# Sub-norm statistics of the second attention by token in columns, and three places changed in the order of a round

## The chip, the cores and the metric

One core of one Trainium2 chip runs the whole kernel. The metric is the device time of one execution in microseconds; before the change the median of three runs is 1058.67 us (1057.43 to 1059.17). The engines are TensorE (PE; its weight loads are shown as PEld), VectorE (DVE), ScalarE (ACT), GpSimd (POOL) and SyncE (SP, which issues all DMAs). Each runs its own instructions in their written order and waits for the others on semaphores, which the kernel places by hand.

## The reference

Two transformer blocks on 512 tokens of width 1024, float32. The change lies in the second block, in the part that mixes two kinds of attention. The differential half has 4 heads of 128 values:

```python
p = jax.nn.softmax(sc, axis=-1)              # two score maps per head
a = p[:, :, 0] - lam * p[:, :, 1]            # causal, with ALiBi slopes
d_out = einsum('bhqk,bhkd->bhqd', a, v)
d_out = rms_norm(d_out, diff_subln) * (1.0 - lambda_init)   # over the 128 values of a head, eps 1e-6
d_out = d_out * silu(dg)
```

The other half (8 "moba" heads of 64 values; with 512 tokens its block choice falls away and it is plain causal softmax attention) has no such norm: its output is `softmax(...) v * silu(mg)`. Both are joined and multiplied by `w_out_2`. The norm over a head's 128 values, for each token, is what the kernel below calls the sub-norm.

## The kernel before, in words

Activations lie transposed: features on the 128 partitions, the 512 tokens along the free side. Each float32 product is made of three products of split numbers (high and low parts; L442 to L444), so one "piece" of a projection is three matmuls of 128x512. Weights come in units of 128x1024; for each unit ACT makes the high part (L1047), POOL the low part (L2173), PE then multiplies 8 pieces.

The second attention goes over 8 chunks c = 0 to 7 of 128 features. Even chunks are differential heads (two score maps, "head" 0 and 1 of the code, joined into one before the values), odd chunks are two moba heads. A round of the main loop takes an even chunk c and the odd chunk c + 1 and prepares c + 2: three full rounds (c = 0, 2, 4), and then a tail in which chunk 6 and 7 end beside the first pieces of the output projection (`out_chunks`). A round lasts some 42 us. No planner orders the work: each engine's block writes its order out by hand, and the loops `for c in range(0, KC, 2)` of PE, ACT, DVE and POOL are the four queues that the change touches.

What they do for a chunk:
- `scores2(c, part)` on PE makes the scores in three parts, `biased(c, part)` on DVE adds the slopes and takes the row maximum (L1994, L1997), `exponentials(c, part)` on ACT (L1413) takes the exponentials in place in `s2` and their sums in `den`.
- Even chunks only: `joined(c, blocks)` on DVE (L2007, L2009, L2014) adds the second map, times a factor by token, to the first.
- `transposes(c, head)` on PE (L870) turns the probabilities into bank PT; `high_probs` (ACT, L1425) and `low_probs` (DVE, L1566) split them; `values2(c, head)` on PE multiplies them with the values into bank OUT.
- Even chunks then: `raw_out` on DVE copies bank OUT into `att2`, `square_out` on ACT squares it into `d_sq`. `square_sum(c)` on PE sums the squares over the 128 partitions with a matrix of ones (L931), which leaves the sum in every partition of bank OUT, and adds the epsilon term, spread as `rx_d`, with four more products by the identity (L933). `variance` on DVE copies that to `d_v`, `first_root` on ACT takes exp(-0.5 ln v) (L1445, L1447), `root` on DVE makes one Newton step and the scaling (four operations, L1562, L2088, L2091, L2094), all on 128x512. POOL multiplies by the gate (`gated_out`, L2347) and later makes the low part of the result (`mixed_low`).
- Odd chunks: `den_rows` on PE (L902) spreads the reciprocal sums into bank PT, `gate_row` on DVE multiplies them into the gate, `gated` gives the output.
- The gate of chunk c is a projection of 8 pieces (`gate_part`), drained by DVE (`gate2_drain`), clamped by POOL (L2336), its sigmoid made by ACT (L1431 to L1435) and multiplied by POOL (`gate_silu`, L2341).

The order of a round around the change, before it. PE: transposes(c+1, 0), square_sum(c), half of value projection c+3, scores2(c+2, 0), transposes(c+1, 1), scores2(c+2, 1), other half of value projection, scores2(c+2, 2), values2(c+1, 0), 5 gate pieces, values2(c+1, 1), den_rows(c+1), 3 gate pieces, and then transposes(c+2) of the next round, which wait for `joined(c+2)`. DVE: variance(c), low_probs(c+1, 0), biased(c+2, 0), biased(c+2, 1), value_drain(c+3), root(c), biased(c+2, 2), low_probs(c+1, 1), joined (two blocks), gate_row(c+1), joined (two blocks), gate2_drain(c+2). ACT: high_probs(c+1, 0), gate_sigmoid(c+1), a weight unit, gate_sigmoid(c), exponentials(c+2, 0), first_root(c), exponentials(c+2, 1). POOL, unchanged: gate_silu(c+1), the low part of a weight unit, gate_silu(c), and then gated_out(c), which waits for `root(c)`.

The arrays `ncol` (128x4x4), `den`, `rden`, `fac`, `rx_d`, `d_sq`, `att2`, `s2` lie in SBUF, `ps` is PSUM. `V.wait()` makes DVE wait for its own last recorded instruction.

Of the kernel before, what the change touches and what calls it, by code (L numbers as in the profile page):

```python
# [14 lines left out]
P = 128  # L15
# [63 lines left out]
def two_layer_block(nc, xT, vecs, wstream, outT):  # L79
    with ExitStack() as ctx:  # L80
# [161 lines left out]
        def out_weights(t):  # L242
# [46 lines left out]
            sem("out_read"), sem("raw_copied"), sem("dsq_ready"), sem("dss_ready"), sem("dvar_ready"),  # L289
            sem("drs_ready"), sem("d_final"), sem("att2_final"), sem("mixed_ready"))  # L290
        pool_held, gap_zeroed = sem("pool_held"), sem("gap_zeroed")
        stored = sem("stored")
# [146 lines left out]
        def _(pe):  # L439
# [433 lines left out]
            def values2(c, head=0):  # L873
# [8 lines left out]
                if head == 0:  # L882
                    pe.wait_ge(v2_lo_ready, max(c + 1, 2))
                    if not is_diff(c):
                        pe.wait_ge(gap_zeroed, 2)
                        pe.wait_ge(dvar_ready, c // 2 + 1)
                    elif c:
                        pe.wait_ge(out_read, c // 2)
# [8 lines left out]
            def den_rows(c):  # L897

                pe.wait_ge(rx_ready, c + 1)
                pe.wait_ge(ptl_ready, tq_of(c, 1) + 1)  # L900
                for b in range(TB):
                    mm = pe.transpose(ps[:, PT_BANK, b * P:(b + 1) * P], rx_m[:, b, :], ident[:, :])  # L902
                mm.then_inc(row2_ready, 1)
# [21 lines left out]
            def square_sum(c):  # L925

                if c >= KC:
                    return
                pe.wait_ge(dsq_ready, c // 2 + 1)
                pe.wait_ge(rx_ready, c + 1)  # L930
                pe.matmul(ps[:, OUT_BANK, :], ones[:, :], d_sq[:, :], start=True, stop=False, skip_group_check=True)  # L931
                for b in range(TB):
                    mm = pe.matmul(ps[:, OUT_BANK, b * P:(b + 1) * P], rx_d[:, b, :], ident[:, :], start=False,  # L933
                                   stop=b == TB - 1, skip_group_check=True)
                mm.then_inc(dss_ready, 1)

            def out_chunks(t, first, last):
# [46 lines left out]
            for c in range(0, KC, 2):  # L984
# [19 lines left out]
                if c + 2 < KC:  # L1004
                    square_sum(c)
                    value_half(c + 3, 0)
                    scores2(c + 2, 0)
                    transposes(c + 1, 1)
                    scores2(c + 2, 1)
                    value_half(c + 3, 1)  # L1010
                    scores2(c + 2, 2)
                    values2(c + 1, 0)
                    gate_part(c + 2, 0, 5)
                    values2(c + 1, 1)
                    den_rows(c + 1)
                    gate_part(c + 2, 5, KC)

            square_sum(KC - 2)
            pe.wait_ge(g_drained, KC)
            out_chunks(0, 0, KC - 2)  # L1020
            transposes(KC - 1, 1)
            values2(KC - 1, 0)
# [16 lines left out]
        def _(act):  # L1039
# [402 lines left out]
            def first_root(c):  # L1442

                act.wait_ge(dvar_ready, c // 2 + 1)
                A.do(act.activation(d_y[:, :], d_v[:, :], ACT.Ln))  # L1445
                A.wait()
                act.activation(d_y[:, :], d_y[:, :], ACT.Exp, scale=-0.5).then_inc(drs_ready, 1)  # L1447

# [48 lines left out]
            for c in range(0, KC - 2, 2):  # L1497
                if c:
                    high_probs(c - 1, 1)
                    exponentials(c, 2)  # L1500
                    high_mixed(c - 2)
                    split_unit(v_unit(c + 2))
                    split_unit(g_unit(c + 1))
                    stage_v2(c + 1)
# [11 lines left out]
                high_probs(c + 1, 0)  # L1516
                gate_sigmoid(c + 1)
                split_unit(g_unit(c + 2))
                gate_sigmoid(c)
                exponentials(c + 2, 0)  # L1520
                first_root(c)
                exponentials(c + 2, 1)
                stage_qk2(c + 3)

            high_probs(KC - 3, 1)
            exponentials(KC - 2, 2)
            split_unit(g_unit(KC - 1))
# [8 lines left out]
            square_out(KC - 2)  # L1536
            high_probs(KC - 1, 0)
            gate_sigmoid(KC - 2)
            split_unit(U_W2 + 1)
            first_root(KC - 2)  # L1540
            gate_sigmoid(KC - 1)
# [11 lines left out]
        def _(dve):  # L1553
# [465 lines left out]
            def den_small(c):  # L2019
# [4 lines left out]
                if is_diff(c):  # L2024
                    V.do(dve.scalar_tensor_tensor(out=den[:, 0, 0, :], in0=den[:, 0, 0, :], scalar=P * EPS, in1=den[:, 0, 0, :],
                                                  op0=ALU.mult, op1=ALU.mult))
# [3 lines left out]
            def den_spread(c):  # L2030
# [4 lines left out]
                dve.wait_ge(nb_used, 16)  # L2035
                if is_diff(c):
                    r = den[:, 0, 0, :].rearrange("p (b o) -> p b o", o=1).to_broadcast([P, TB, P])
                    dve.tensor_copy(rx_d[:, :, :], r).then_inc(rx_ready, 1)
                else:
                    r = den[:, 1, :, :].rearrange("p h (b o) -> p b h o", o=1).to_broadcast([P, TB, 2, 64])  # L2040
                    dve.tensor_copy(by_heads(rx_m[:, :, :]), r).then_inc(rx_ready, 1)

# [36 lines left out]
            def variance(c):  # L2079

                dve.wait_ge(dss_ready, c // 2 + 1)
                ts(d_v[:, :], ps[:, OUT_BANK, :], 1.0 / P, ALU.mult).then_inc(dvar_ready, 1)

            def root(c):

                dve.wait_ge(drs_ready, c // 2 + 1)
                V.do(tt(d_sq[:, :], d_y[:, :], d_y[:, :], ALU.mult))
                V.do(dve.scalar_tensor_tensor(out=d_y[:, :], in0=att2[:, 0, :], scalar=small[:, 7:8], in1=d_y[:, :],  # L2088
                                              op0=ALU.mult, op1=ALU.mult))
                V.wait(back=1)  # L2090
                V.do(dve.scalar_tensor_tensor(out=d_sq[:, :], in0=d_sq[:, :], scalar=-0.5, in1=d_v[:, :],  # L2091
                                              op0=ALU.mult, op1=ALU.mult))
                V.wait()
                dve.scalar_tensor_tensor(out=att2[:, 0, :], in0=d_sq[:, :], scalar=1.5, in1=d_y[:, :],  # L2094
                                         op0=ALU.add, op1=ALU.mult).then_inc(d_final, 1)

# [30 lines left out]
            for c in range(0, KC, 2):  # L2127
# [4 lines left out]
                den_small(c)  # L2132
                den_spread(c)
                biased(c + 1, 1)
# [11 lines left out]
                variance(c)  # L2146
                low_probs(c + 1, 0)
                biased(c + 2, 0)
                biased(c + 2, 1)
                value_drain(c + 3)  # L2150
                root(c)
                biased(c + 2, 2)
                low_probs(c + 1, 1)
                joined(c + 2, (3, 2))
                gate_row(c + 1)
                joined(c + 2, (0, 1))
                gate2_drain(c + 2)
# [344 lines left out]
```

## Time and profile before

| | |
|---|---|
| median of three runs | 1058.67 us |
| time of the profiled execution | 1057.33 us |
| its span (first to last instruction) | 1055.5 us |
| PE busy | 1032.9 us, 98% of the span |
| DVE, ACT, POOL busy | 514.8, 458.9, 516.1 us |
| granted clock of PE, mean | 1.00 |
| chain that ended last, share of PE | 87% |
| DMA | 91.03 MB, mean 86 GB/s |

PE is the engine to look at; the others are busy for about half of the span. The starts of two neighbouring rows of a timeline give what the first cost the engine; the durations of matmuls overlap. The profiled time is 1.83 us above its span, and the median is 1.34 us above the profiled time. Times in a timeline are microseconds from the start of the span.

### The profile page before, as it was taken

The numbers are of one execution on the slowest core, as the hardware profiler recorded it, in microseconds if no ns is written. First come the engines' busy times: TensorE is split into PE (matmuls) and PEld (weight loads), VectorE is DVE, ScalarE is ACT, GpSimd is POOL, SyncE is SP. The second block draws the span as 40 slices with busy tenths as digits, with TensorE's granted clock in tenths as the row PEclk, the third lists the DMA queues.
The fourth block names the chain that finished last, engine by engine and source line by source line (L and its number), as shares of the span: only waits on it lengthen the run. The fifth ranks groups of instructions, "written<-read, shape, count | busy, mean of one in ns | idle before, by whom it ended". The sixth has DMA issues, their size and how long they took to land.

```text
span 1055.5 us, 13360 instructions
## 1 busy us (share of the span) xinstructions
PE 1032.9 (98%) x4926; PEld 849.3 (80%) x4926; DVE 514.8 (49%) x833; ACT 458.9 (43%) x667; POOL 516.1 (49%) x300
## 2 busy tenths in 40 slices
PE   7999999999999999999999999999999999999998
PEld 5888887788888787888888888887888877777787
DVE  6899763544362465343434311003624176675731
ACT  5322345788753334332323322223353357476540
POOL 3444554933434514444444446445276544675562
PEclk9999999999999999999999999999999999999999
DMA  7233231112142312232222323334122211111112
GB/s 241 87 100 100 80 100 40 60 41 80 61 158 97 124 40 80 99 99 98 88 93 99 99 100 104 109 106 139 41 80 79 81 61 41 61 45 56 40 60 80
DMA packets 25965, 91.03 MB, mean 86 GB/s; under 512 B 3008, under 2 KB 3136, under 8 KB 25792
## 3 DMA queue, kind: packets, MB, share of 16 engines
q1 hardware_dynamic: 25920, 90.42, 25.5%
q8 instruction: 30, 0.49, 0.2%
q14 instruction: 15, 0.12, 0.0%
HBM read 88.31 MB, written 2.10 MB: 86 GB/s over the span
## 4 chain that ended last, share of the span: by engine, by line
PE 87%; DVE 5%; issue 3%; ACT 3%; POOL 1%; DMA 0%; SPq 0%; POOLq 0%; DVEq 0%; ACTq 0%
PE ps L442 26%; PE ps L443 25%; PE ps L444 25%; PE ps L846 1%; PE ps L870 1%; POOL w_lo L2173 1%; DVE s L2014 1%; PE ps L484 1%; PE ps L568 1%; PE ps L588 1%; DVE sp L1687 1%; ACT soft L1137 1%; ACT soft L1135 1%; PE ps L582 1%; ACT soft L1133 1%
## 5 line engine op out<-in xcount | busy, mean ns | idle before, releaser
L2173 POOL TENSOR_TENSOR w_lo<-w_raw,w_hi 128x1024 fp32r<-128x1024 f32 x146 | 346.9, 2377 | 428.2 <-ACT w_hi L1047 379.0
L1047 ACT ACTIVATE w_hi<-w_raw 128x1024 fp32r<-128x1024 f32 (+1 forms) x140 | 146.4, 1045 | 290.1 <-PE ps L444 290.0
L442 PE MATMUL ps<-a_hi,w_hi 128*128 128x512 f32 x560 | 223.4, 399 | 13.0 <-DVE w_lo L1566 7.2
L444 PE MATMUL ps<-a_hi,w_lo 128*128 128x512 f32 x560 | 219.0, 391 | 0.0
L443 PE MATMUL ps<-a_lo,w_hi 128*128 128x512 f32 x560 | 218.8, 391 | 0.0
L442 PE MATMUL ps<-b_hi,w_hi 128*128 128x512 f32 x408 | 159.3, 391 | 1.1 <-POOL w_lo L2173 0.8
L444 PE MATMUL ps<-b_hi,w_lo 128*128 128x512 f32 x408 | 158.8, 389 | 0.0
L443 PE MATMUL ps<-b_lo,w_hi 128*128 128x512 f32 x408 | 158.7, 389 | 0.0
L442 PEld LDWEIGHTS ps<-a_hi,w_hi 128*128 128x128 f32 x560 | 105.6, 189 | 39.0 <-issue 8.7
L444 PEld LDWEIGHTS ps<-a_hi,w_lo 128*128 128x128 f32 x560 | 105.5, 188 | 22.7
L443 PEld LDWEIGHTS ps<-a_lo,w_hi 128*128 128x128 f32 x560 | 105.7, 189 | 20.7
L442 PEld LDWEIGHTS ps<-b_hi,w_hi 128*128 128x128 f32 x408 | 76.6, 188 | 17.7 <-POOL w_lo L2173 1.2
L443 PEld LDWEIGHTS ps<-b_lo,w_hi 128*128 128x128 f32 x408 | 76.6, 188 | 15.8
L444 PEld LDWEIGHTS ps<-b_hi,w_lo 128*128 128x128 f32 x408 | 76.6, 188 | 15.8
L1649 DVE SCALAR_TENSOR_TENSOR ps<-u_pad,vec,ps 128x512 f32<-128x512 f32 x112 | 75.5, 748 | 0.0
L442 PE MATMUL ps<-h_hi,w_hi 128*128 128x512 f32 x176 | 68.5, 389 | 0.0
L443 PE MATMUL ps<-h_lo,w_hi 128*128 128x512 f32 x176 | 68.5, 389 | 0.0
L444 PE MATMUL ps<-h_hi,w_lo 128*128 128x512 f32 x176 | 68.5, 389 | 0.0
L1562 DVE TENSOR_TENSOR up_h<-up_u,up_s 128x512 f32<-128x512 f32 x22 | 49.5, 2248 | 21.5 <-ACT up_s L1306 21.3
L1562 DVE TENSOR_TENSOR up_u<-ps,scale_row 128x512 f32<-128x512 f32 x22 | 15.2, 690 | 83.4 <-PE ps L444 83.4
L1562 DVE TENSOR_TENSOR sq_f<-sq_f 128x512 f32<-128x512 f32 x13 | 9.8, 751 | 82.5 <-ACT sq_f L1330 81.9
L1413 ACT ACTIVATE s<-s,smax 128x384 f32<-128x384 f32 (+2 forms) x64 | 35.2, 552 | 17.2 <-DVE smax L1997 17.2
(324 smaller groups left out, 1600.1 us busy)
## 6 DMA issues: line engine op xcount, KB each, us to landing
w_raw<-weights SPq DMA_DIRECT2D x159, 512.0 KB, 3.3
resid<-x_t SPq DMA_DIRECT2D x8, 256.0 KB, 5.6
resid<-x_t SPq DMA_DIRECT2D x1, 2048.0 KB, 9.5
out_t<-out_sb SPq DMA_DIRECT2D x8, 256.0 KB, 2.0
w_raw<-weights SPq DMA_DIRECT2D x2, 256.0 KB, 4.6
vec<-vecs SPq DMA_DIRECT2D x1, 220.0 KB, 8.2
vec<-vecs SPq DMA_DIRECT2D x1, 4.0 KB, 1.8
```

Of the source, the lines that this page charges most:

```text
L442: pe.matmul(out, s_hi, m_hi, start=first, stop=False, skip_group_check=True)
L443: pe.matmul(out, s_hi, m_lo, start=False, stop=False, skip_group_check=True)
L444: return pe.matmul(out, s_lo, m_hi, start=False, stop=last, skip_group_check=True)
L484: pe.matmul(ps[:, 5, :], tri[:, :], src, start=True, stop=True, skip_group_check=True)
L568: pe.matmul(z_of(h)[:, o:o + (TB - j) * P], k[r, key], q[r, j * P:T], start=j != 3 and t == 0, stop=False, skip_group_check=True)
L582: pe.matmul(z[:, w], tri[:, :], parts[:, w], start=False, stop=False, skip_group_check=True)
L588: mm = pe.matmul(z[:, o:o + width], neg_ones[:, :], parts[:, Z_COL[j2]:Z_COL[j2] + width], start=False, stop=False, skip_group_check=True)
L1047: act.activation(w_hi[:, k % 2, 0:width], w_raw[:, k, 0:width], ACT.Copy).then_inc(hi_ready, 1)
L1413: e = act.activation(s2[:, head, w], s2[:, head, w], ACT.Exp, scale=-1.0, bias=smax[:, head, b:b + 1], accum_out=den[:, kind_of(c), half_o ...
L1562: return dve.tensor_tensor(out, in0, in1, op)
L1649: V.do(dve.scalar_tensor_tensor(out=acc if k == TAPS - 1 else part, in0=src, scalar=w, in1=part, op0=ALU.mult, op1=ALU.add))
L2173: pool.tensor_tensor(w_lo[:, k % 2, 0:width], w_raw[:, k, 0:width], w_hi[:, k % 2, 0:width].bitcast(F32), ALU.subtract).then_inc(lo_ready, 1)
```

## The change

The sub-norm's statistics are kept by token in columns. The squares become the stationary operand of four products with one column of ones, which leaves the sum of token 128b + p in partition p, column b. `variance` adds the epsilon term from `den` there, ACT's two operations and DVE's Newton step work on 128x4 columns in `ncol`, a copy spreads the result to 128x512 in `rx_d`, and a new `norm_row` on PE transposes it back to a row in bank OUT, behind transposes(c+1, 1). A new `scaled_out` on DVE multiplies. values2(c+1, 0) now waits for that product, since the row lies in bank OUT.

The order changes in four places: ACT's first_root goes ahead of the weight unit and gate_sigmoid(c); DVE's root goes ahead of biased(c+2, 0); the third part of the exponentials goes ahead of high_probs(c+1, 1), and the first half of joined(c+2) ahead of low_probs(c+1, 1), the second half ahead of gate_row; and 6 instead of 5 gate pieces stand between the two values2.

```diff
--- before.py
+++ after.py
@@ -288,6 +288,7 @@
         out_read, raw_copied, dsq_ready, dss_ready, dvar_ready, drs_ready, d_final, att2_final, mixed_ready = (
             sem("out_read"), sem("raw_copied"), sem("dsq_ready"), sem("dss_ready"), sem("dvar_ready"),
             sem("drs_ready"), sem("d_final"), sem("att2_final"), sem("mixed_ready"))
+        dr_ready, drow_ready = sem("dr_ready"), sem("drow_ready")
         pool_held, gap_zeroed = sem("pool_held"), sem("gap_zeroed")
         stored = sem("stored")
 
@@ -883,7 +884,7 @@
                     pe.wait_ge(v2_lo_ready, max(c + 1, 2))
                     if not is_diff(c):
                         pe.wait_ge(gap_zeroed, 2)
-                        pe.wait_ge(dvar_ready, c // 2 + 1)
+                        pe.wait_ge(d_final, c // 2 + 1)
                     elif c:
                         pe.wait_ge(out_read, c // 2)
                 pe.wait_ge(ptl_ready, tq + 1)
@@ -896,7 +897,7 @@
 
             def den_rows(c):
 
-                pe.wait_ge(rx_ready, c + 1)
+                pe.wait_ge(rx_ready, c // 2 + 1)
                 pe.wait_ge(ptl_ready, tq_of(c, 1) + 1)
                 for b in range(TB):
                     mm = pe.transpose(ps[:, PT_BANK, b * P:(b + 1) * P], rx_m[:, b, :], ident[:, :])
@@ -927,12 +928,17 @@
                 if c >= KC:
                     return
                 pe.wait_ge(dsq_ready, c // 2 + 1)
-                pe.wait_ge(rx_ready, c + 1)
-                pe.matmul(ps[:, OUT_BANK, :], ones[:, :], d_sq[:, :], start=True, stop=False, skip_group_check=True)
                 for b in range(TB):
-                    mm = pe.matmul(ps[:, OUT_BANK, b * P:(b + 1) * P], rx_d[:, b, :], ident[:, :], start=False,
-                                   stop=b == TB - 1, skip_group_check=True)
+                    mm = pe.matmul(ps[:, OUT_BANK, b:b + 1], d_sq[:, b * P:(b + 1) * P], ones[:, 0:1], start=b == 0, stop=True,
+                                   skip_group_check=True)
                 mm.then_inc(dss_ready, 1)
+
+            def norm_row(c):
+
+                pe.wait_ge(dr_ready, c // 2 + 1)
+                for b in range(TB):
+                    mm = pe.transpose(ps[:, OUT_BANK, b * P:(b + 1) * P], rx_d[:, b, :], ident[:, :])
+                mm.then_inc(drow_ready, 1)
 
             def out_chunks(t, first, last):
 
@@ -1006,18 +1012,20 @@
                     value_half(c + 3, 0)
                     scores2(c + 2, 0)
                     transposes(c + 1, 1)
+                    norm_row(c)
                     scores2(c + 2, 1)
                     value_half(c + 3, 1)
                     scores2(c + 2, 2)
                     values2(c + 1, 0)
-                    gate_part(c + 2, 0, 5)
+                    gate_part(c + 2, 0, 6)
                     values2(c + 1, 1)
                     den_rows(c + 1)
-                    gate_part(c + 2, 5, KC)
+                    gate_part(c + 2, 6, KC)
 
             square_sum(KC - 2)
             pe.wait_ge(g_drained, KC)
             out_chunks(0, 0, KC - 2)
+            norm_row(KC - 2)
             transposes(KC - 1, 1)
             values2(KC - 1, 0)
             pe.wait_ge(s2_biased, 4 * 16)
@@ -1442,9 +1450,9 @@
             def first_root(c):
 
                 act.wait_ge(dvar_ready, c // 2 + 1)
-                A.do(act.activation(d_y[:, :], d_v[:, :], ACT.Ln))
+                A.do(act.activation(ncol[:, 1, :], ncol[:, 0, :], ACT.Ln))
                 A.wait()
-                act.activation(d_y[:, :], d_y[:, :], ACT.Exp, scale=-0.5).then_inc(drs_ready, 1)
+                act.activation(ncol[:, 1, :], ncol[:, 1, :], ACT.Exp, scale=-0.5).then_inc(drs_ready, 1)
 
             def high_mixed(c):
                 if is_diff(c):
@@ -1496,8 +1504,8 @@
             split_unit(v_unit(3))
             for c in range(0, KC - 2, 2):
                 if c:
+                    exponentials(c, 2)
                     high_probs(c - 1, 1)
-                    exponentials(c, 2)
                     high_mixed(c - 2)
                     split_unit(v_unit(c + 2))
                     split_unit(g_unit(c + 1))
@@ -1515,15 +1523,15 @@
                 stage_v2(c + 2)
                 high_probs(c + 1, 0)
                 gate_sigmoid(c + 1)
+                first_root(c)
                 split_unit(g_unit(c + 2))
                 gate_sigmoid(c)
                 exponentials(c + 2, 0)
-                first_root(c)
                 exponentials(c + 2, 1)
                 stage_qk2(c + 3)
 
+            exponentials(KC - 2, 2)
             high_probs(KC - 3, 1)
-            exponentials(KC - 2, 2)
             split_unit(g_unit(KC - 1))
             stage_v2(KC - 1)
             high_mixed(KC - 4)
@@ -1535,9 +1543,9 @@
             exponentials(KC - 1, 2)
             square_out(KC - 2)
             high_probs(KC - 1, 0)
+            first_root(KC - 2)
             gate_sigmoid(KC - 2)
             split_unit(U_W2 + 1)
-            first_root(KC - 2)
             gate_sigmoid(KC - 1)
             high_probs(KC - 1, 1)
             for t in (2, 3):
@@ -2022,7 +2030,7 @@
                     return
                 dve.wait_ge(p2_exp, 2 * c + 2)
                 if is_diff(c):
-                    V.do(dve.scalar_tensor_tensor(out=den[:, 0, 0, :], in0=den[:, 0, 0, :], scalar=P * EPS, in1=den[:, 0, 0, :],
+                    V.do(dve.scalar_tensor_tensor(out=den[:, 0, 0, :], in0=den[:, 0, 0, :], scalar=EPS, in1=den[:, 0, 0, :],
                                                   op0=ALU.mult, op1=ALU.mult))
                 else:
                     V.do(dve.reciprocal(den[:, 1, :, :], den[:, 1, :, :]))
@@ -2033,12 +2041,8 @@
                     return
                 V.wait()
                 dve.wait_ge(nb_used, 16)
-                if is_diff(c):
-                    r = den[:, 0, 0, :].rearrange("p (b o) -> p b o", o=1).to_broadcast([P, TB, P])
-                    dve.tensor_copy(rx_d[:, :, :], r).then_inc(rx_ready, 1)
-                else:
-                    r = den[:, 1, :, :].rearrange("p h (b o) -> p b h o", o=1).to_broadcast([P, TB, 2, 64])
-                    dve.tensor_copy(by_heads(rx_m[:, :, :]), r).then_inc(rx_ready, 1)
+                r = den[:, 1, :, :].rearrange("p h (b o) -> p b h o", o=1).to_broadcast([P, TB, 2, 64])
+                dve.tensor_copy(by_heads(rx_m[:, :, :]), r).then_inc(rx_ready, 1)
 
             def low_probs(c, head=0):
                 if c >= KC:
@@ -2078,21 +2082,30 @@
 
             def variance(c):
 
+                V.wait()
                 dve.wait_ge(dss_ready, c // 2 + 1)
-                ts(d_v[:, :], ps[:, OUT_BANK, :], 1.0 / P, ALU.mult).then_inc(dvar_ready, 1)
+                dve.scalar_tensor_tensor(out=ncol[:, 0, :], in0=ps[:, OUT_BANK, 0:TB], scalar=1.0 / P, in1=den[:, 0, 0, :],
+                                         op0=ALU.mult, op1=ALU.add).then_inc(dvar_ready, 1)
 
             def root(c):
 
+                v, y, t = ncol[:, 0, :], ncol[:, 1, :], ncol[:, 2, :]
                 dve.wait_ge(drs_ready, c // 2 + 1)
-                V.do(tt(d_sq[:, :], d_y[:, :], d_y[:, :], ALU.mult))
-                V.do(dve.scalar_tensor_tensor(out=d_y[:, :], in0=att2[:, 0, :], scalar=small[:, 7:8], in1=d_y[:, :],
-                                              op0=ALU.mult, op1=ALU.mult))
-                V.wait(back=1)
-                V.do(dve.scalar_tensor_tensor(out=d_sq[:, :], in0=d_sq[:, :], scalar=-0.5, in1=d_v[:, :],
-                                              op0=ALU.mult, op1=ALU.mult))
+                V.do(tt(t, y, y, ALU.mult))
                 V.wait()
-                dve.scalar_tensor_tensor(out=att2[:, 0, :], in0=d_sq[:, :], scalar=1.5, in1=d_y[:, :],
-                                         op0=ALU.add, op1=ALU.mult).then_inc(d_final, 1)
+                V.do(dve.scalar_tensor_tensor(out=t, in0=t, scalar=-0.5, in1=v, op0=ALU.mult, op1=ALU.mult))
+                V.wait()
+                V.do(dve.scalar_tensor_tensor(out=y, in0=t, scalar=1.5, in1=y, op0=ALU.add, op1=ALU.mult))
+                V.wait()
+                dve.wait_ge(nb_used, 16)
+                r = y.rearrange("p (b o) -> p b o", o=1).to_broadcast([P, TB, P])
+                dve.tensor_copy(rx_d[:, :, :], r).then_inc(dr_ready, 1)
+
+            def scaled_out(c):
+
+                dve.wait_ge(drow_ready, c // 2 + 1)
+                dve.scalar_tensor_tensor(out=att2[:, 0, :], in0=att2[:, 0, :], scalar=small[:, 7:8], in1=ps[:, OUT_BANK, :],
+                                         op0=ALU.mult, op1=ALU.mult).then_inc(d_final, 1)
 
             for u in range(4, 9):
                 query_drain(u)
@@ -2130,7 +2143,6 @@
                 if c:
                     value_drain(c + 2)
                 den_small(c)
-                den_spread(c)
                 biased(c + 1, 1)
                 if 0 < c < KC - 2:
                     biased(c + 1, 2)
@@ -2145,15 +2157,16 @@
                 value_low(c + 2)
                 variance(c)
                 low_probs(c + 1, 0)
+                root(c)
                 biased(c + 2, 0)
                 biased(c + 2, 1)
+                scaled_out(c)
                 value_drain(c + 3)
-                root(c)
                 biased(c + 2, 2)
+                joined(c + 2, (3, 2))
                 low_probs(c + 1, 1)
-                joined(c + 2, (3, 2))
+                joined(c + 2, (0, 1))
                 gate_row(c + 1)
-                joined(c + 2, (0, 1))
                 gate2_drain(c + 2)
                 slopes(c + 3)
                 value_low(c + 3)
```

## Rows read from the trace of the kernel before

**Rows 1.** Busy time by stretch: PE, PEld, DVE, ACT, POOL, granted clock, DMA share, GB/s.
```profile
920.00:940.00 20.00, 20.00 (x122) 16.22 (x121) 14.54 (x39) 16.24 (x33) 12.28 (x12) 1.00 0.08 27
```

**Rows 2.** Waits of PE, 840 to 1056 us: in total, times, longest.
```profile
PE ps L870 <- DVE s L2014: 3.0, 3, 1.6
```

**Rows 3.** Timeline of PE: start, us, operation, [idle before, releaser].
```profile
921.48 1.25 PE L870 MATMUL ps<-ident,s 128*128 128x128 f32 x10
922.62 1.12 PE L931 MATMUL ps<-d_sq,ones 128*128 128x512 f32 x2
...
924.40 0.48 PE L442 MATMUL ps<-a_hi,w_hi 128*128 128x512 f32 x1
...
928.24 1.31 PE L870 MATMUL ps<-ident,s 128*128 128x128 f32 x10
929.48 0.44 PE L846 MATMUL ps<-k_hi,q_hi 64*128 64x384 f32 x2
...
941.28 0.62 PE L902 MATMUL ps<-ident,rx_m 128*128 128x128 f32 x4
...
944.66 1.31 PE L870 MATMUL ps<-ident,s 128*128 128x128 f32 x10 [0.69 <-DVE s L2014]
```

**Rows 4.** Timeline of PE at the feed-forward norm.
```profile
728.85 0.95 PE L471 MATMUL ps<-ones,sq_f 128*128 128x1 f32 x8
729.66 1.19 PE L484 MATMUL ps<-h_hi,tri 128*128 128x512 f32 x4
```

**Rows 5.** Timeline of ACT in the same round as group 3.
```profile
925.93 1.04 ACT L1047 ACTIVATE w_hi<-w_raw 128x1024 fp32r<-128x1024 f32 x1
```

**Rows 6.** Groups of ACT by line: busy us, mean ns, idle before.
```profile
L1055 ACT ACTIVATE ncol<-ps 128x4 f32<-128x4 f32 x5 | 0.9, 174 | 15.3 <-DVE ps L1559 15.3
```

**Rows 7.** Timeline of DVE in the same round.
```profile
928.47 0.69 DVE L1997 CUSTOM_DVE_ANT_0 s<-ps,bias_h 128x512 f32<-128x512 f32 x1
...
934.14 0.68 DVE L1562 TENSOR_TENSOR d_sq<-d_y 128x512 f32<-128x512 f32 x1
...
939.09 0.22 DVE L2009 SCALAR_TENSOR_TENSOR fac<-rden,small,den 128x4 f32<-128x4 f32 x1
```

**Rows 8.** Timeline of POOL in the same round.
```profile
926.19 1.30 POOL L2341 TENSOR_TENSOR gate_e<-gate_g,gate_e 128x512 f32<-128x512 f32 x1
927.45 2.38 POOL L2173 TENSOR_TENSOR w_lo<-w_raw,w_hi 128x1024 fp32r<-128x1024 f32 x1
929.79 1.29 POOL L2341 TENSOR_TENSOR gate_e<-gate_g,gate_e 128x512 f32<-128x512 f32 x1
936.95 1.30 POOL L2347 TENSOR_TENSOR att<-att,gate_e 128x512 f32<-128x512 f32 x1 [5.87 <-DVE att L2094]
```

**Rows 9.** Timeline of DVE, last join (round of chunk 4).
```profile
980.76 0.59 DVE L2009 SCALAR_TENSOR_TENSOR fac<-rden,small,den 128x4 f32<-128x4 f32 x1
981.38 4.56 DVE L2014 SCALAR_TENSOR_TENSOR s<-s,fac 128x512 f32<-128x512 f32 x2
```

**Rows 10.** Timeline of POOL in that stretch.
```profile
980.02 1.31 POOL L2321 TENSOR_TENSOR q_lo<-y_qk,q_hi 128x512 fp32r<-128x512 f32 x1
...
981.42 1.30 POOL L2321 TENSOR_TENSOR k_lo<-y_qk,k_hi 128x512 fp32r<-128x512 f32 x1
982.66 2.86 POOL L2173 TENSOR_TENSOR w_lo<-w_raw,w_hi 128x1024 fp32r<-128x1024 f32 x1
```

**Rows 11.** Timeline of DVE in the tail (chunk 6).
```profile
1006.52 2.11 DVE L1562 TENSOR_TENSOR d_sq<-d_y 128x512 f32<-128x512 f32 x1 [0.94 <-ACT d_y L1447]
```

**Rows 12.** Timeline of POOL in the tail.
```profile
1005.69 2.40 POOL L2363 TENSOR_TENSOR w_lo<-w_raw,w_hi 128x1024 fp32r<-128x1024 f32 x1
```

**Rows 13.** One line's instructions: ns min/median/max, first and last start.
```profile
L2041 DVE COPY rx_m<-den x4: 426/862/1241, 880.3 to 1000.9; 128x512 f32<-128x512 f32 x4
```

**Rows 14.** Timeline of PE at the kernel's start.
```profile
7.25 0.77 PE L442 MATMUL ps<-a_hi,w_hi 128*128 128x512 f32 x1 [7.25 <-DVE w_lo L1566]
...
10.80 0.51 PE L444 MATMUL ps<-a_hi,w_lo 128*128 128x512 f32 x1
```

## Prediction

> **What bounds the kernel now.** I read the busy time by stretch first: in 20 us of the loop PE is busy for all of them, at a granted clock of 1.00, its upper level of 2.4 GHz, while DVE, ACT and POOL work 14.5, 16.2 and 12.3 us [rows 1]. So an edit pays only where it takes work from PE or closes a hole in PE's queue, and costs where it makes one. Then the waits of PE: the transposes that open a round stood 3.0 us in three times, at most 1.6, for the join [rows 2]; one is 0.69 us [rows 3], which leaves 0.7 for the third. The timelines of the four engines over the round of chunk 2 (902.96 to 944.66 us) show the rest. The others repeat it about 41.7 us earlier and later, with the same order on POOL.
>
> **PE's work.** Before, the square sum costs 924.40 - 922.62 = 1.78 us between neighbouring starts [rows 3]. After, it is four products of a 128x128 stationary with one column. The same form at the feed-forward norm costs 729.66 - 728.85 = 0.81 us [rows 4]. The new norm_row is four transposes; ten cost 922.62 - 921.48 = 1.14 us, so four cost 0.46 [rows 3]. PE is relieved of 1.78 - 0.81 - 0.46 = 0.51 us each time, four times: 2.0 us. The sixth gate piece only changes sides.
>
> **The hole ahead of transposes(c+2).** The first half of the join now stands ahead of low_probs and its exponentials ahead of high_probs, so `joined` finishes some 2 to 4 us before PE's last gate pieces; I expect its 3.0 us [rows 2] gone. The next to be late would be the gate row, which must have read bank PT: den_rows ends 0.62 us after its start at 941.28 [rows 3], the product takes 0.68 (estimate, from the 128x512 product of [rows 7]), together 1.30 + 0.1 for two hand-overs; PE has 0.46 us of den_rows and two pieces at 0.69, 1.84 us. It fits by some 0.4 us. Price if this cover fails: the overshoot, up to 0.7 us a round. The same for low_probs(c+1, 1), which now stands behind half a join: the sixth piece gives PE 0.69 us more, so I cost it at nothing for chunks 0 and 2 and at 0.1 for chunk 4, where POOL's q_lo and k_lo run beside the join [rows 10]; at worst it costs one blocked operation, 1.3 us.
>
> **The wait that I think decides: root.** Before, root(c) runs at 934.14 [rows 7], in a stretch of 5.87 us in which POOL does nothing but wait for it [rows 8]. After, it stands ahead of biased(c+2, 0), and PE's norm_row waits for it in order, with scores2(c+2, 1) behind.
>
> When it may start: first_root takes the weight unit's place at 925.93 [rows 5]; two operations on 128x4 at 0.174 [rows 6] and hand-overs end at 926.35. DVE has done low_probs by then.
>
> What POOL does then: gate_silu(c+1) 926.19 to 927.49, the low part of a weight unit 927.45 to 929.83, gate_silu(c) 929.79 to 931.08, without a hole [rows 8]. Their inputs move by 0.3 us and stay in time (the unit's high part then ends at 927.35).
>
> What that does to DVE: root is now three operations with all inputs in SBUF, `ncol`, and a copy from SBUF to SBUF. The trace has the forms beside a busy POOL. The product d_sq, two inputs in SBUF, took 2.11 instead of 0.68 us [rows 7, 11]: it started at 1006.52 while POOL's w_lo ran from 1005.69 to 1008.09 [rows 12] and ended 0.54 after it. Small ones are held too: `fac` on 128x4 took 0.59 instead of 0.22 us [rows 7, 9], to the end of q_lo (981.33) [rows 10]. The operation behind it was ready 0.03 us later, and POOL's next had the turn: the two of the join took 4.56 us, ending 0.42 after w_lo, which itself was drawn out to 2.86 [rows 9, 10]. So DVE gets one such operation in between two of POOL. The SBUF copy shows both faces: 0.43 and 1.24 us [rows 13].
>
> The Trainium skill's page "SBUF — State Buffer", section "Who interferes with whom", states this as a rule: a VectorE instruction with two inputs in SBUF, or a copy in a two-port mode, and a GpSimd instruction that reads SBUF block each other for a whole instruction. The trace agrees (2.11 against 0.68 us); by the rule too this change is slower, and without it it would be faster.
>
> Counted out: operation 1 goes at 927.5, behind gate_silu(c+1); 2 behind w_lo; 3 behind gate_silu(c), whose end is now about 931.2; then POOL waits for scaled_out and the copy runs free: 0.1 + 0.1 + 0.45, the row is ready at 931.85. PE would like to start norm_row at 928.24 - (1.78 - 0.81) + (929.48 - 928.24) = 928.51 [rows 3]. So PE stands for 3.3 us. Behind the copy DVE does the first of biased(c+2, 0), 0.69 long [rows 7]; scores2(c+2, 1) waits for that and starts at 932.5, against 929.48 before [rows 3]: 3.0 us late. Behind biased stand the exponentials and the next parts, whose chain now has the length that it has in the trace, so they come as late as PE and no later. scaled_out stands in DVE's hole behind biased(c+2, 1), far ahead of values2(c+1, 0): nothing. POOL's gated_out moves with it, and in chunks 0 and 2 it is idle when the join's first half comes.
>
> Bounds of root, from its start at 926.35: free of POOL it takes 4 x 0.22 + 0.3, ready at 927.5, ahead of PE's 928.51, so no stall at all; at the other end each of POOL's three operations also waits out one of DVE's (some 0.1 to 0.2 us each), ready at 932.2; gated_out can't hold the copy, since it waits for scaled_out. The value is near the upper end, by the row of `fac`, the nearest in size and form.
>
> **The sum.** A round that starts scores2(c+2, 1) 3.0 us late and no longer has its hole: chunk 0, 3.0 - 0.7 = +2.3; chunk 2, +2.3; chunk 4, 3.0 + 0.1 - 1.6 = +1.5. Chunk 6 in the tail: root comes at about 1004.2, where POOL waits for the gate's sigmoid, and norm_row has six output pieces (4.1 us) ahead of it; no stall, -0.5. Together +5.6 us: 1057.33 + 5.6 = 1062.9 by the profiled execution, and against the median, 1.34 above it, 1064.3 us.
>
> **The rivals.**
> *DVE is not held* (the other side: faster). The operations are so short that they slip in between POOL's, or the columns do not need the contested path. Then -2.0 of PE work and -3.0 of holes: 1053.7 us. It decides where root is ready before 928.51, that is where at most the first of the four waits. For it: only 0.37 us of delay was seen on a small one, once. Against it: that 0.37 was all that was left of q_lo. Chance 0.18.
> *DVE slips in twice.* Operations 1 and 2 go between gate_silu(c+1) and w_lo, or the copy right behind operation 3, so that gate_silu(c) is not waited for. The row is ready some 1.3 us sooner, scores2 is 1.7 us late: +1.0, +1.0, +0.2, -0.5 = +1.7: 1060.4 us. Against it: `fac` and its follower, 0.03 us apart, did not get in together [rows 9, 10]. Chance 0.11.
> *PE's clock falls after the stall.* The kernel's first matmuls, after PE had stood for 7.25 us, came 0.44 us apart (8 from 7.25 to 10.80) [rows 14], against 0.23 later: the lower level, 1.2 GHz, for 3.55 us, 1.6 us lost. Three times that is +4.8: 1069.1 us. Chance 0.11. The Trainium skill's "TensorE: Matmul & The Clock Gate", section "Why this matters for your kernels", advises against idle gaps of about this length; no row here shows one in mid-kernel.
> *The change misses its aim elsewhere*: the join is still late, or the gate row. That would add 0.7 to 2 us a round to either side and lies inside the ranges.
>
> **How the numbers follow.** The forecast has 0.60, with a range of its own from 1061.5 to 1067. About 0.2% (2.1 us, so 1056.6 to 1060.8) is what this kernel's measurement can tell from no change. Slower: 0.60 + 0.11 and a little of the third case, 0.72; same: most of the double slip, 0.10; faster: 0.18. The range for 8 in 10 takes in the falling clock above, 1070, and reaches down past the double slip to the edge of the free case, 1054.5.
>
> **What would show it.** In the new profile: DVE's three operations on `ncol` take 1 to 2.4 us each instead of 0.2, ending with POOL's w_lo and gate_silu; PE stands some 3 us before the transposes of `rx_d`, released by DVE, three times, and not in the tail; the waits on the join are gone; products with one column 0.81 us, transposes 0.46; rounds of some 44 us (43.2 for chunk 4) instead of 41.7. Wrong if those operations take 0.2 us each while POOL is busy: then PE has no holes and the time falls to about 1054. Half right if one of them waits and the rest don't.

## The result, and the profile after

The changed kernel takes 1066.87 us (median of four runs, 1065.49 to 1069.06) against 1058.87 us (the three runs of before and one more): ratio 1.0078, 95% interval 1.0063 to 1.0093, 8.0 us slower. Its profiled execution took 1066.63 us with a span of 1064.9; the execution before, 1057.33 with 1055.5.

The nine traces of this case reach the second attention's loop at times between 867.6 and 870.5 us of the span, and what spreads them lies far ahead of the change. One part is PE's first matmuls, which lie 0.43 us apart until about 11 us in the kernel before and until 13.7 us in the first experiment below. The other is a hole of 2.17 us that every trace has at about 196 us. In five traces (before and after among them) the granted clock stayed up behind it, in four it fell. So below I compare the stretches from the loop on. The hole in the kernel before, and the granted clock behind it there and in the first experiment (which reaches that hole 1.4 us later):

```profile
195.83 0.50 PE L442 MATMUL ps<-a_hi,w_hi 128*128 128x512 f32 x1 [2.17 <-DVE g_hi L1562]
...
198.00:200.00 2.00, 2.00 (x10) 1.67 (x9) 0.00 (x0) 1.94 (x3) 2.00 (x2) 1.00 0.00 0
...
198.00:200.00 2.00, 2.00 (x6) 1.58 (x5) 0.00 (x0) 1.97 (x3) 2.00 (x1) 0.50 0.00 0
```

The four stretches of the loop, each from one `transposes` of an even chunk to the next (starts of the rows of that line; the last one to the end of the span), in us:

| kernel | chunk 0 | chunk 2 | chunk 4 | chunk 6 to the end | sum |
|---|---|---|---|---|---|
| before | 35.14 | 41.70 | 42.59 | 68.25 | 187.68 |
| after | 38.52 | 45.03 | 45.48 | 68.09 | 197.12 |
| difference | +3.38 | +3.33 | +2.89 | -0.16 | +9.44 |

All of the loss lies in the three full rounds. Lines of code have moved by one to thirteen: L870 is L871, L2173 is L2186. The waits of PE from 840 us on, to be held against [rows 2]:

```profile
PE ps L940 <- DVE rx_d L2102: 6.7, 3, 2.6
PE ps L443 <- DVE v_lo L1574: 1.5, 3, 0.5
PE ps L443 <- DVE vd_lo L1574: 1.5, 3, 0.7
...
PE ps L443 <- DVE pt_lo L1574: 0.2, 1, 0.2
```

The wait for the join is gone. In its place PE waits for `rx_d` three times, and two small new waits have come. VectorE's timeline in the round of chunk 2 (it starts 3.34 us later than before):

```profile
929.67 1.10 DVE L1570 TENSOR_TENSOR ncol<-ncol 128x4 f32<-128x4 f32 x1 [0.65 <-ACT ncol L1455]
930.80 2.29 DVE L2096 SCALAR_TENSOR_TENSOR ncol<-ncol 128x4 f32<-128x4 f32 x1
933.13 1.19 DVE L2098 SCALAR_TENSOR_TENSOR ncol<-ncol 128x4 f32<-128x4 f32 x1
934.35 0.43 DVE L2102 COPY rx_d<-ncol 128x512 f32<-128x512 f32 x1
```

and POOL beside it, which answers to [rows 8]:

```profile
929.46 1.29 POOL L2354 TENSOR_TENSOR gate_e<-gate_g,gate_e 128x512 f32<-128x512 f32 x1
930.71 2.36 POOL L2186 TENSOR_TENSOR w_lo<-w_raw,w_hi 128x1024 fp32r<-128x1024 f32 x1
933.05 1.25 POOL L2354 TENSOR_TENSOR gate_e<-gate_g,gate_e 128x512 f32<-128x512 f32 x1
939.53 1.29 POOL L2360 TENSOR_TENSOR att<-att,gate_e 128x512 f32<-128x512 f32 x1 [5.23 <-DVE att L2107]
```

The three operations on 128x4 end at 930.77, 933.09 and 934.32, each within 0.02 us of the end of one of POOL's (930.75, 933.07, 934.30); in the rounds of chunks 0 and 4 it is the same, within 0.03 us. Two more rows of this kernel show what is held and what isn't. In the tail, with POOL idle, the same three operations take 0.15 to 0.16 us. And `variance`, whose inputs lie one in PSUM and one in SBUF and whose output lies in SBUF, takes 0.15 us in the middle of one of POOL's operations (VectorE, POOL, then VectorE in the tail):

```profile
927.48 0.15 DVE L2087 SCALAR_TENSOR_TENSOR ncol<-ps,den 128x4 f32<-128x4 f32 x1
...
926.57 1.52 POOL L2334 TENSOR_TENSOR q_lo<-y_qk,q_hi 128x512 fp32r<-128x512 f32 x1
...
1013.60 0.15 DVE L1570 TENSOR_TENSOR ncol<-ncol 128x4 f32<-128x4 f32 x1
1013.78 0.16 DVE L2096 SCALAR_TENSOR_TENSOR ncol<-ncol 128x4 f32<-128x4 f32 x1
1013.98 0.16 DVE L2098 SCALAR_TENSOR_TENSOR ncol<-ncol 128x4 f32<-128x4 f32 x1
```

PE around its stall, and a piece behind it:

```profile
927.62 0.50 PE L443 MATMUL ps<-a_hi,w_hi 128*128 128x512 f32 x1 [0.66 <-DVE vd_lo L1574]
...
934.84 0.66 PE L940 MATMUL ps<-ident,rx_d 128*128 128x128 f32 x4 [2.07 <-DVE rx_d L2102]
935.45 0.45 PE L847 MATMUL ps<-k_hi,q_hi 64*128 64x384 f32 x2
...
938.02 0.63 PE L445 MATMUL ps<-a_hi,w_lo 128*128 128x512 f32 x1
938.45 0.63 PE L443 MATMUL ps<-a_hi,w_hi 128*128 128x512 f32 x1
```

scores2(c+2, 1) starts 29.15 us after its round, against 26.52 before [rows 3]: 2.63 us late (2.66 in chunk 0, 2.88 in chunk 4). And behind the stall neighbouring matmuls start 0.43 us apart, not 0.23. The granted clock by stretch says the same (columns as in [rows 1]); 0.50 is the lower level of 1.2 GHz. It is still 1.00 while PE stands, and falls after that:

```profile
930.00:932.00 2.00, 2.00 (x14) 1.22 (x13) 1.97 (x2) 1.94 (x4) 2.00 (x2) 1.00 0.00 0
932.00:934.00 2.00, 0.77 (x8) 0.53 (x5) 1.97 (x2) 0.44 (x1) 2.00 (x2) 1.00 0.00 0
934.00:936.00 2.00, 1.16 (x8) 0.97 (x10) 1.97 (x8) 0.57 (x1) 0.30 (x1) 0.94 0.75 260
936.00:938.00 2.00, 2.00 (x12) 1.72 (x11) 0.81 (x9) 1.10 (x5) 0.00 (x0) 0.50 0.01 2
938.00:940.00 2.00, 2.00 (x8) 1.61 (x7) 1.38 (x8) 1.93 (x8) 0.47 (x1) 0.71 0.00 0
940.00:942.00 2.00, 2.00 (x13) 1.38 (x12) 0.95 (x3) 0.31 (x1) 0.82 (x1) 1.00 0.00 0
```

### The profile page after: what moved, and what is told of

It is laid out like the page before. It is cut to its first block, busy times and chain, and to the rows that moved or that the text cites. A ratio compares the mean times of both kernels' runs of the same rounds, so it can differ in the third digit from the quotient of the medians.

```text
span 1064.9 us, 13376 instructions
## 1 busy us (share of the span) xinstructions
PE 1036.7 (97%) x4934; PEld 853.6 (80%) x4934; DVE 513.4 (48%) x833; ACT 455.5 (43%) x667; POOL 515.1 (48%) x300
## 4 chain that ended last, share of the span: by engine, by line
PE 86%; DVE 5%; ACT 4%; issue 3%; POOL 1%; DMA 0%; SPq 0%; POOLq 0%; ACTq 0%; DVEq 0%
PE ps L443 27%; PE ps L444 26%; PE ps L445 26%; PE ps L847 1%; POOL w_lo L2186 1%; PE ps L485 1%; PE ps L569 1%; PE ps L589 1%; DVE sp L1695 1%; DVE ncol L2096 1%; ACT soft L1143 1%; ACT soft L1145 1%; PE ps L583 1%; ACT soft L1141 1%; PE ps L871 1%
## 5 line engine op out<-in xcount | busy, mean ns | idle before, releaser
L2186 POOL TENSOR_TENSOR w_lo<-w_raw,w_hi 128x1024 fp32r<-128x1024 f32 x146 | 346.5, 2374 | 438.5 <-ACT w_hi L1055 389.3
```

The costliest lines, as they stand in the source:

```text
L2186: pool.tensor_tensor(w_lo[:, k % 2, 0:width], w_raw[:, k, 0:width], w_hi[:, k % 2, 0:width].bitcast(F32), ALU.subtract).then_inc(lo_ready, 1)
```

## The experiments

**The columns in PSUM.** `variance` writes to, and the Newton step works in, spare columns of the bank that holds the sums; nothing moves in a queue. Each small operation keeps one input in SBUF. The first product becomes v times y instead of y times y. The fence leaves out where `variance` writes, what ScalarE reads, and that the copy reads r.

```diff
-                v, y, t = ncol[:, 0, :], ncol[:, 1, :], ncol[:, 2, :]
+                v, t, r = (ps[:, OUT_BANK, n * TB:(n + 1) * TB] for n in (1, 2, 3))
+                y = ncol[:, 1, :]
-                V.do(tt(t, y, y, ALU.mult))
-                V.do(dve.scalar_tensor_tensor(out=t, in0=t, scalar=-0.5, in1=v, ...))
-                V.do(dve.scalar_tensor_tensor(out=y, in0=t, scalar=1.5, in1=y, ...))
+                V.do(tt(t, v, y, ALU.mult))
+                V.do(dve.scalar_tensor_tensor(out=t, in0=t, scalar=-0.5, in1=y, ...))
+                V.do(dve.scalar_tensor_tensor(out=r, in0=t, scalar=1.5, in1=y, ...))
```

> The changed kernel with the columns' variance, Newton scratch and result in spare columns of the PSUM bank that holds the sums, so that none of the three small operations has two inputs in SBUF and the spread copies from PSUM; nothing moves in any queue. Port theory (an operation with two SBUF inputs or an SBUF to SBUF copy waits out POOL's whole instruction): each of the three takes 0.15 to 0.2 us, the spread 0.45 to 0.7, the row is ready ahead of PE, the three stalls of 2.1 to 2.6 us go, and PE's clock stays at 1.00 in every stretch: 3.3 x 3 of stall and holes plus 1.6 x 3 of slow clock are not all on top of each other in the trace (1064.9 us of span now); I expect a span near 1053.5 and a median near 1055.5 us, faster than both kernels. Rival (the operations are slow for their place in the queue, or for hand-overs between dependent operations): no change, 1065 to 1067 us.

Measured: 1056.34 us median of 8, ratio to before 0.9973 (0.9963 to 0.9984). VectorE's timeline in the same place of its round:

```profile
927.98 0.17 DVE L1570 TENSOR_TENSOR ps<-ps,ncol 128x4 f32<-128x4 f32 x1 [0.62 <-ACT ncol L1455]
928.18 0.17 DVE L2097 SCALAR_TENSOR_TENSOR ps<-ps,ncol 128x4 f32<-128x4 f32 x1
928.38 0.17 DVE L2099 SCALAR_TENSOR_TENSOR ps<-ps,ncol 128x4 f32<-128x4 f32 x1
928.59 0.69 DVE L2103 COPY rx_d<-ps 128x512 f32<-128x512 f32 x1
```

Three operations at 0.17 us beside the same busy POOL, no wait of PE for `rx_d`, a granted clock of 1.00 from 880 us on. So the wait goes with where the operands lie, and that turns 8 us lost into 2.5 us won. Outputs have moved here as well as inputs; the row of `variance` above, with its output in SBUF, says that it is the inputs. That the contested thing is a port is the theory's name for it; the runs show only who waits for whom. The expected 1055.5 was 0.8 too low; PE still waits 1.5 us for `vd_lo` (below).

**POOL's operation made short.** The changed kernel, with the low part of the weight unit between the two gate products cut to 128 of its 1024 columns; the rest of that low part is left out.

```diff
-                low_unit(g_unit(c + 2))
+                low_weights(g_unit(c + 2) // 4, g_unit(c + 2) % 4, UNIT // 8)
```

> The changed kernel with POOL's low part of the gate's weight unit cut to an eighth of its width in the three rounds, between the two gate products (the low part of the rest is left out, so the output is not the reference's). Port theory: the second Newton operation takes some 0.5 us instead of 2.3, the row comes 2.0 us sooner, PE's stalls shrink from 2.1 to 2.6 us to 0.1 to 0.6 each, the clock no longer falls; 3 x (2.0 + 1.6) = 10.8 us at most, so a median of 1056 to 1058 us. Rival (hand-overs or queue order): the operation keeps its 2.3 us and the time stays at 1065 to 1067 us.

Measured: 1055.85 us median of 7, ratio 0.9972 (0.9961 to 0.9983), 0.15 below the expected range. In VectorE's timeline the second operation shrank with POOL's, from 2.29 to 0.38 us; the first kept its length:

```profile
927.75 1.10 DVE L1570 TENSOR_TENSOR ncol<-ncol 128x4 f32<-128x4 f32 x1 [0.65 <-ACT ncol L1455]
928.88 0.38 DVE L2096 SCALAR_TENSOR_TENSOR ncol<-ncol 128x4 f32<-128x4 f32 x1
929.30 0.16 DVE L2098 SCALAR_TENSOR_TENSOR ncol<-ncol 128x4 f32<-128x4 f32 x1
```

POOL's part took 0.45 us (928.79 to 929.24), and since POOL then stood until 930.59 for the next sigmoid, the third was free too. PE's stall is gone altogether, where I had left 0.1 to 0.6 us of it. So here an operation on 128x4 costs what POOL happens to be doing.

**Filler in the stall.** The changed kernel, with products that write to the bank that the row overwrites.

```diff
             def norm_row(c):
+                if c < KC - 2:
+                    pe.wait_ge(dvar_ready, c // 2 + 1)
+                    for _ in range(11):
+                        pe.matmul(ps[:, OUT_BANK, :], a_hi[:, 0, 0:P], a_hi[:, 0, :], start=True, stop=True, ...)
```

> The changed kernel with 11 products of 128x512 in front of norm_row in each of the three rounds, which write to the bank that the row will overwrite; they stand only for PE's activity while it waits. Clock theory (the stall lets the clock fall to its lower level, which then costs its own time): the granted clock stays at 1.00 behind the stall, matmuls there stay 0.23 us apart, DVE's waits are unchanged, and the time falls by up to 1.6 us a round, to some 1062 to 1063 us, at 3 x 0.1 us less if the filler overshoots. Rival (the stretch behind the stall is slow for another reason, such as waits on the delayed DVE chain): no change or slower, 1067 to 1068 us.

Measured: 1062.88 us median of 4, ratio 1.0044 (1.0029 to 1.0060). VectorE's three operations are as long as in the changed kernel (1.11, 2.31, 1.21 us in this round); the rounds are 1.51, 1.29 and 1.24 us shorter. PE's timeline, with the filler in the place of the stall and matmuls 0.23 us apart behind the row:

```profile
931.19 2.78 PE L941 MATMUL ps<-a_hi 128*128 128x512 f32 x11
933.81 0.60 PE L944 MATMUL ps<-ident,rx_d 128*128 128x128 f32 x4
...
935.93 0.39 PE L445 MATMUL ps<-a_hi,w_lo 128*128 128x512 f32 x1
936.16 0.39 PE L443 MATMUL ps<-a_hi,w_hi 128*128 128x512 f32 x1
```

The granted clock of that stretch, to be held against 0.50 in the changed kernel:

```profile
936.00:938.00 2.00, 2.00 (x11) 1.62 (x9) 1.72 (x10) 1.81 (x7) 0.14 (x1) 1.00 0.00 0
```

The rounds gained a little less than the clock cost, since the filler ends after the row is ready: from the start of the copy of `rx_d` to norm_row it is 0.76 us in chunks 2 and 4 (933.05 to 933.81), 0.49 in the changed kernel. Counted from norm_row to the next round, the stretches are 1.58, 1.63 and 1.56 us shorter. So about 4.8 of the 9.44 us are the clock that fell after each stall, and the other 4.7 the stall itself less what the change saves.

**The order alone.** The kernel before with the exponentials and the join a place forward and six gate pieces; VectorE's part of the edit:

```diff
-                low_probs(c + 1, 1)
                 joined(c + 2, (3, 2))
-                gate_row(c + 1)
+                low_probs(c + 1, 1)
                 joined(c + 2, (0, 1))
+                gate_row(c + 1)
```

> The kernel before with the order alone: third exponentials ahead of high_probs, half of the join ahead of low_probs, the other half ahead of gate_row, six gate pieces; statistics and root as before. If the order alone closes the holes: 3.0 us less, 1055.8 us. My own expectation: root still stands in front of the join with 2.6 us of DVE, so low_probs comes some 1.4 us late for the second values in each round, and the gain is about used up: 1057 to 1060 us, PE waiting for pt_lo instead of for the join.

Measured: 1066.81 us median of 4, ratio 1.0075 (1.0060 to 1.0091), 7 us above the range that I expected. Chunks 0 and 2 did as expected (PE waits 1.27 us for `pt_lo`, the join's 0.7 is gone, the rounds are 0.6 us longer). In chunk 4 the join ran into POOL's q_lo, k_lo and w_lo again, as in [rows 9, 10], but now with low_probs behind it (VectorE's timeline):

```profile
983.47 1.12 DVE L2009 SCALAR_TENSOR_TENSOR fac<-rden,small,den 128x4 f32<-128x4 f32 x1
984.63 4.48 DVE L2014 SCALAR_TENSOR_TENSOR s<-s,fac 128x512 f32<-128x512 f32 x2
989.04 1.48 DVE L1566 TENSOR_TENSOR pt_lo<-ps,pt_hi 128x1280 fp32r<-128x1280 f32 x1
```

and PE's second values, which wait for it:

```profile
990.57 0.80 PE L442 MATMUL ps<-pt_hi,v_hi 128*128 128x512 f32 x1 [5.37 <-DVE pt_lo L1566]
```

PE stood for 5.37 us, the clock fell again (0.50 from 990 to 994 us), and that round took 6.07 us more than before. I had those three POOL operations in my rows and did not count them for this kernel.

**The statistics alone**, with the order of before:

> The changed kernel with the order of the kernel before for exponentials, join and gate pieces. Port theory: the stall and the falling clock come from root alone, so the time is the changed kernel's, 1066 to 1068 us, with the same three small operations at 1.1 to 2.3 us. Rival (the bundle of order edits brings the loss): back to 1055 to 1059 us.

Measured: 1069.23 us median of 4, ratio 1.0093 (1.0077 to 1.0110), 1.2 above the expected range, the small operations at 1.10, 2.29 and 1.19 us. PE waits for the join again, 1.4 us in two, which I had not added. The loss is there without the order edits, and they save some 1.9 us beside it (198.97 against 197.12 for the loop). The four executions spread from 1066.34 us, at a mean granted clock of 0.998, to 1070.56 at 0.993: the lower the mean clock, the longer the time.

**The PSUM form with the order of before:**

> The PSUM form of the first experiment with the order of the kernel before for exponentials, join and gate pieces (five): columns and early root alone. With root out of the way of the join, DVE has 2.6 us less in front of it, so if that alone closed the holes, the time equals the first experiment's, 1056.3 us. If the order edits are needed for a part of them, PE waits again for the join, mostly in chunk 4's round, and the time is 0.3 to 1.5 us higher. I expect the first for chunks 0 and 2 and about 0.5 us for chunk 4: 1056.8 us.

Measured: 1057.84 us median of 11, ratio 0.9987 (0.9978 to 0.9996), 1.0 above what I expected. Its waits show again

```profile
PE ps L871 <- DVE s L2022: 1.4, 2, 0.7
```

By the loop, the order edits are worth 186.78 - 185.16 = 1.6 us with the PSUM form. I had it the wrong way round: with root moved, the join is in time in chunk 4 and late by 0.70 us in chunks 0 and 2.

**The PSUM form with a free VectorE ahead of `vd_lo`:**

```diff
                 den_small(c + 1)
-                den_spread(c + 1)
+                value_low(c + 2)
                 slopes(c + 2)
-                value_low(c + 2)
 ...
                 biased(c + 2, 1)
+                den_spread(c + 1)
                 scaled_out(c)
```

> The PSUM form of the first experiment, and on VectorE value_low(c+2) ahead of slopes(c+2), with den_spread(c+1), an SBUF to SBUF copy that POOL's b_lo holds for 1.24 us there, moved to behind biased(c+2, 1), where POOL is idle. If the new hole ahead of value_half(c+3, 0) (0.16, 0.66 and 0.66 us) is that held copy's: vd_lo comes 1.0 to 1.4 us sooner, the holes go, 1.3 to 1.5 us less than the first experiment's 1056.3: 1054.9 us. If it is ACT's vd_hi instead, which comes after two other operations: the holes shrink to 0.2 to 0.4 us and the median is 1055.5 us.

Measured: 1053.92 us median of 5, ratio 0.9958 (0.9944 to 0.9971), the fastest of all, below both of the expected times. The hole before value_half is down to 0.5 us over the three rounds, and the spread of `rx_m`, 1.24 us long before root, takes 0.42 in its new place. The wait of PE, and that copy in VectorE's timeline:

```profile
PE ps L443 <- DVE vd_lo L1574: 0.5, 3, 0.2
```

```profile
930.99 0.42 DVE L2045 COPY rx_m<-den 128x512 f32<-128x512 f32 x1
```

What is left of the hole is released by ACT's `vd_hi`, on which VectorE now waits 1.07 us. This is the second of the two expected cases. The loop takes 184.11 us, 1.05 less than without these two moves. The medians differ by more, 2.4 us, and the ratios to before by 0.15%, 1.6 us; but three of the five executions here had a mean granted clock of 1.000 and three of the eight in the first experiment, and these differ by 1.2 us (1053.66 to 1053.92 against 1055.00 to 1055.11).

## Why the prediction was right, and where its size was off

**Root and the port: right, in mechanism and nearly in size.** The order of the waits came as counted: the first operation behind gate_silu(c+1), the second behind the weight unit, the third behind gate_silu(c), the copy free. Taken back by the 3.34 us that the round starts later, the row was ready at 931.44 (forecast 931.85) and scores2(c+2, 1) started at 932.11 (932.5): 2.63 us late, not 3.0. The two experiments on operands and on POOL's length show the cause, and so does the tail, where the same operations beside an idle POOL took 0.15 to 0.16 us; hand-overs and queue order are ruled out.

**The clock: the term that was mis-sized.** I gave a falling clock 0.11 and treated it as an alternative to the forecast; it came on top of it, three times in three stalls of 2.05 to 2.55 us. The price was right, 1.56 to 1.63 us each against 1.6 (its own rows give 3.55 - 8 x 0.23 = 1.7). Of the 9.44 us that the loop lost, 4.8 are this term, which the sum had at nothing, and 4.7 are what the sum had at +5.6. The profiled executions differ by 9.3 us and the medians by 8.0. That the median, 1066.87, still lies inside the forecast's own range, 0.13 us from its end, is partly luck: the 4.8 us that the sum had left out were offset by 0.9 us too much in the rest and by 1.4 us less between the medians than in the loop.

The Trainium skill's "TensorE: Matmul & The Clock Gate", section "Why this matters for your kernels", warns of idle gaps longer than these; here 2.05 us were enough, and the measurement decides. My reading that no row of the kernel before shows such a hole in mid-kernel was wrong: its trace has one of 2.17 us at 195.83, behind which the clock did not fall, while behind the same hole it fell in four other traces. So at about 2 us the clock may fall and may not, and one trace doesn't tell. What decides it stays open.

**PE's work: less than counted.** Products and transposes cost 0.92 and 0.43 us (1010.95 to 1011.87 and 1016.08 to 1016.51 in the tail), not 0.81 and 0.46: 0.43 saved each time, 1.7 us instead of 2.0. Of that, a step that I missed took 0.16, 0.66 and 0.66 us back: value_half(c+3, 0) waits for `vd_lo`. The long square sum had covered that; a shorter one uncovers it, and 1.5 of the 1.7 us are gone. I had looked for what is late next behind the join and not behind the sum.

**The hole at the join: right.** 3.0 us gone, no new wait at the gate row. low_probs in chunk 4 came 0.22 us late, 0.1 was forecast. In the tail 0.16 us were won instead of 0.5; PE took 1.21 us instead of 1.01 from transposes(7, 1) to values2(7, 0), which now waits for scaled_out. I did not test whether that is the reason.

**The rivals.** *Not held* and *slips in twice* are out: three of three were held, and never two of root's between two of POOL's. The price of the first, 1053.7 us, was too low: with the operands out of POOL's way it was 1056.3, and its loop was 2.5 us shorter than before, not 5.0. Most of the difference is the wait on `vd_lo`, 1.5 us, and 0.3 that PE's work saves less.

## What to carry to other kernels

Before a small VectorE step is moved or made smaller, look at what POOL does at its new place: in this kernel an operation with two inputs in SBUF, and an SBUF copy, waited out POOL's current instruction, even at 128x4, and a dependent chain paid one POOL instruction for each link while POOL's queue was full. One of the two inputs in PSUM took it out of the way. Not every operation on SBUF is held: the reciprocal of `den`, with one input there, took 0.19 us beside a busy POOL (925.10 in the changed kernel). And when a piece of PE work shrinks, look at what it covered, and price a stall of PE with the slow clock behind it, not only with its own length.

## What the runs showed of the hardware that I had not expected

The first operation multiplies a column by itself, one tensor as both inputs, and was held all the same, 1.10 us instead of the 0.15 of the tail. PE's clock fell after 2.05 us of standing, and behind one hole of 2.17 us in four traces out of nine, while in the loops of these traces it fell behind no hole of 0.5 to 1.6 us (clock 1.00 from 980 to 1000 us in the kernel before, with its 1.60 us hole).

And the two bundled edits, which each lose when made alone, 7.9 us (the order) and 10.1 us (the statistics) against the runs beside them, lose 8.0 together, so they can't be added. The order alone loses in chunk 4, where low_probs stands behind a join that has the old root in front of it; with root moved away, low_probs is 0.22 us late there, not 5.37.
